# A decoder step on one core: mask DMAs issued from SyncE instead of GpSimd, and the sample attention placed later between the weight blocks

## The reference

```python
h = rmsnorm(x, g_mix); z = h @ w_in                   # q, k, v of three mixers, and merge gates
ya = mlstm(...)                                       # 4 heads
# B: dilated window attention, 3 groups x 2 heads; C: block-sparse attention, 6 heads
s = einsum('bthd,btjhd->bthj', q, keys) * Dh ** -0.5
s = where(idx >= 0, s + bias, -inf)                   # T5 bias by distance
p, lse = softmax_lse(s)
o = einsum('bthj,btjhd->bthd', p, values)
y = ga * (ya @ wa) + gb * (yb @ wb) + gc * (yc @ wc)  # ga, gb, gc = sigmoid(gates)
x = x + y @ w_out
x = x + (silu(a) * u) @ w_dn                          # a, u = split(rmsnorm(x) @ w_gu)
return rmsnorm(x, g_final)
```

## Time and profile before

| what | value |
|---|---|
| median of three runs | 1018.16 us |
| the profiled execution | 1017.9 us |
| its span, first to last instruction | 1016.0 us |
| outside the span | 1.9 us |
| PE busy | 994.9 us (98%) |
| weight loads on PE | 961.2 us (95%) |
| DVE, ACT, POOL busy | 49%, 34%, 7% |
| granted TensorE clock | 0.998 |
| mean DMA rate | 103 GB/s |

### The profile page before, as it was taken

One profiled execution on the slowest core, in us unless ns is written; L12 is line 12 of the kernel. 1 busy time (PEld: TensorE's weight loads), 2 busy tenths in 40 slices (PEclk: granted clock), 3 DMA queues, 4 the chain that ended last, 5 costly groups with the idle time before them and its releaser, 6 DMA issues.

```text
span 1016.0 us, 18552 instructions
## 1 busy us (share of the span) xinstructions
PE 994.9 (98%) x7715; PEld 961.2 (95%) x7715; DVE 494.5 (49%) x903; ACT 344.7 (34%) x579; POOL 69.1 (7%) x95
## 2 busy tenths in 40 slices
PE   6999999999999999999999999999999999999997
PEld 6799989998998889999999999999999999999997
DVE  5525456565587313263536556455545554332232
ACT  6434233444455343222322343232222222222122
POOL 0100014001100200020204000000000000000000
PEclk9999999999999999999999999999999999999999
DMA  7574345412121465422222222322222222222202
GB/s 254 166 287 99 48 141 90 166 54 84 56 84 42 127 184 162 125 84 84 84 84 84 84 84 98 103 91 84 84 83 84 83 84 93 94 85 73 91 25 88
DMA packets 104522, 104.17 MB, mean 103 GB/s; under 512 B 10825, under 2 KB 101379, under 8 KB 104199
## 3 DMA queue, kind: packets, MB, share of 16 engines
q1 hardware_dynamic: 101044, 91.94, 29.0%
q0 software_dynamic: 3344, 11.03, 3.3%
q10 hardware_dynamic: 52, 0.01, 0.0%
HBM read 97.16 MB, written 14.88 MB: 110 GB/s over the span
## 4 chain that ended last, share of the span: by engine, by line
PE 91%; DVE 3%; DMA 1%; POOL 1%; SPq 1%; issue 1%; ACT 1%; ACTq 0%; DVEq 0%; POOLq 0%
PE acc L432 75%; PE acc L936 3%; PE acc L916 2%; PE acc L999 2%; PE acc L926 1%; PE acc L1035 1%; POOL mt L751 1%; PE acc L982 1%; SPq L626 1%; PE acc L844 1%; PE acc L833 1%; DVE h_lo L1887 1%; PE acc L799 1%; DMA ring<-in_cache_dsa_kv 1%; DVE y_lo L1539 0%
## 5 line engine op out<-in xcount | busy, mean ns | idle before, releaser
L432 PE MATMUL acc<-h_hi,w_hi 128*128 128x256 f32 (+1 forms) x1520 | 472.3, 311 | 2.6 <-DVE w_lo L416 2.5
L432 PE MATMUL acc<-h_lo,w_hi 128*128 128x256 f32 (+1 forms) x1520 | 438.3, 288 | 0.0
L432 PE MATMUL acc<-h_hi,w_lo 128*128 128x256 f32 (+1 forms) x1520 | 436.7, 287 | 0.0
L432 PEld LDWEIGHTS acc<-h_hi,w_hi 128*128 128x128 f32 x1520 | 286.6, 189 | 13.9 <-issue 6.6
L432 PEld LDWEIGHTS acc<-h_lo,w_hi 128*128 128x128 f32 x1520 | 287.0, 189 | 6.5 <-issue 3.4
L411 ACT ACTIVATE w_hi<-raw 128x1024 fp32r<-128x1024 f32 x135 | 141.4, 1047 | 440.0 <-PE acc L432 439.9
L432 PEld LDWEIGHTS acc<-h_hi,w_lo 128*128 128x128 f32 x1520 | 286.7, 189 | 0.0
L416 DVE TENSOR_TENSOR w_lo<-raw,w_hi 128x1024 fp32r<-128x1024 f32 x135 | 165.4, 1225 | 111.1 <-ACT w_hi L411 106.5
L432 PE MATMUL acc<-s_hi,w_hi 128*128 128x256 f32 (+1 forms) x352 | 101.6, 288 | 0.0
L432 PE MATMUL acc<-s_lo,w_hi 128*128 128x256 f32 (+1 forms) x352 | 101.3, 288 | 0.0
L432 PE MATMUL acc<-s_hi,w_lo 128*128 128x256 f32 (+1 forms) x352 | 100.7, 286 | 0.0
(11 more groups left out here) (303 smaller groups left out, 1165.8 us busy)
## 6 DMA issues: line engine op xcount, KB each, us to landing
raw<-in_w_in SPq DMA_DIRECT2D x25, 1024.0 KB, 5.1
raw<-in_w_gate_up SPq DMA_DIRECT2D x22, 1024.0 KB, 4.9
raw<-in_w_down SPq DMA_DIRECT2D x8, 1024.0 KB, 5.1
ring<-in_cache_dsa_kv SPq DMA_DIRECT2D x4, 1024.0 KB, 6.5
raw<-in_w_out SPq DMA_DIRECT2D x4, 1024.0 KB, 5.0
out<-in_cache_dsa_kv SPq DMA_DIRECT2D x2, 2016.0 KB
rev<-tab POOLq DMA_DIRECT2D x1, 3840.0 KB, 34.7
ring<-in_cache_moba_k SPq DMA_DIRECT2D x48, 64.0 KB, 2.1
```

What stands on the lines that cost most here:

```text
L432: ins = nc.tensor.matmul(acc[:, bank, 0:HALF[half]], a[:, k, :], two(b[:, kx + k, :], half), start=first and k == k0 and c == 0, stop=last ...
```

## The change

Three things. The mask DMAs are issued by SP, between the fourth ring load and the next weight load, instead of by POOL. DVE's three operations that wait for them are due at T_SA + 1.6 instead of T_SA + 3.0. The due times of the sample attention are later and further apart, with those of its ring loads on SP, and the low parts of y have two due times instead of nine.

```diff
-        T_QK, D_QK = 1.3, 0.042
-        T_SM, T_P, D_PV = 3.4, 4.6, 0.05
+        T_QK, D_QK = 1.45, 0.048
+        T_SM, T_P, D_PV = 3.9, 5.05, 0.055
@@ SP
-                    when = (0.4, 0.41, 0.42, 0.43, 1.7, 2.05, 2.35, 2.7, 3.05, 3.4, 4.8, 4.9)
+                    when = (0.4, 0.41, 0.42, 0.43, 1.95, 2.35, 2.75, 3.1, 3.5, 3.85, 5.3, 5.4)
@@ SP, behind the issue of ring load n
+                        if n == 3:
+                            sp.wait_ge(sem("rev_out"), 16)
+                            for head in range(HEADS):
+                                half, q = divmod(head // 2, 3)
+                                w = P * NC4[head // 2]
+                                r0 = HD * half + TS * (head % 2)
+                                src = bass.AP(X["rev"].tensor, REV * head + TP - 1 - w,
+                                              [[4 * HEADS * REV, NB], [HEADS * REV - 1, TB], [1, w + TB]])
+                                sp.dma_start(S4[r0:r0 + TS, q, 2 * P - w:2 * P + TB], src
+                                             ).then_inc(sem("mask_in"), 16)
@@ POOL: the same loop taken out
-                for head in range(HEADS):
-                    ...
-                    pool.dma_start(S4[r0:r0 + TS, q, 2 * P - w:2 * P + TB], src).then_inc(sem("mask_in"), 16)
@@ DVE, merge
-                        yield T_SA + T_P + len(pv) * D_PV + (0.12, 0.12, 0.2, 0.2, 0.21, 0.4, 0.5, 0.6, 0.9)[i]
+                        yield T_SA + T_P + (0.12 if n < 2 else 0.2) + len(pv) * D_PV
@@ DVE, sample
-                    yield T_SA + T_SM - 0.4
+                    yield T_SA + 1.6
                     dve.wait_ge(sem("new_mm"), 1)
                     dve.wait_ge(sem("mask_in"), 16 * HEADS)
```

## The result

The changed kernel took 1031.61 us (median; 1030.99 to 1033.16) against 1018.03 (median of four runs of the kernel before): ratio 1.0138, 95% interval [1.012, 1.0154]. It is slower by 13.6 us, where 6.1 were forecast, and above the range. The direction and each wait's place were as forecast; the size wasn't. Its profiled execution took 1033.77, with a span of 1031.8.

A forecast was written before the change was run, and what follows sets the result against it. PE was taken as the bound (91% of the last-ending chain), its work plus gaps. Terms -0.5 + 5.0 - 1.0 + 0.1 - 0.4 + 3.4 gave +6.6, by position +5.6; +6.1 taken: 1017.9 + 6.1 = 1024.0 us, range 1019 to 1028.5.

The forecast's parts named there:

- the masks on SP: Scores, block 35: masks land at 367.4, so PE stalls before step 19 until 370.2; +5.0 us, bounds 2.0 to 10.1.
- Start, -0.5: First scores step, block 34: moved from place 5 to 8, weight work covers PE's 0.51 us ring-load wait; -0.5 us.
- Wider spacing, -1.0: Scores: 36 places instead of 32 among the steps, fewer steps directly following another; -1.0 us, bounds +0.3 and -4.2.
- Softmax, +0.1: Softmax: weight parts, a Tanh and an evacuation now ahead on ACT and DVE use about 1.3 of 1.6 us cover; +0.1 us.
- Values, -0.4: Products with the values: five places instead of four before the ninth step shorten PE's wait for the twelfth ring load; -0.4 us.
- y, +3.4: Last product with the values to PE's restart on y: chain 7.6 us, PE's work 3.0, gap 4.6 instead of 1.2; +3.4 us.
- What the masks delay on SP, "Nothing": SP's queue behind the masks: weights of blocks 39 and 40 and fifth and sixth ring loads go 5 us later, costing nothing.
- in time: Rival, scores: masks land by 362.4, no stall at step 19; +1.1 us, 1019.0; chance 0.15.
- spacing pays: Rival, scores: every step's key copy is ready and masks are in time; spacing gives -4.2 us, 1015.8; chance 0.07.
- SP is held behind its own loads: Rival, SP's queue: masks meet a hold-up like that behind the fifth ring load, landing 3.7 us later; 1027.7; chance 0.10.

The follow-up runs named there:

- masks_pool: The changed kernel with the twelve mask DMAs back on POOL, due times and early wait kept; 1020.9 us, ratio 1.0023 to the kernel before.
- The run with six masks: The changed kernel with six mask DMAs on SP and six on POOL, DVE waiting for all; 1029.01 us, ratio 1.0086 to the kernel before.
- the filled pair: On one chip, the changed kernel again (1032.84 us) and with 43 and 18 unread identity products in PE's waits for masks and y (1028.88 us).
- the two filled runs: The changed kernel with unread identity products in PE's waits for masks and y: 36 and 16 (1027.01 us), then 43 and 18 (1028.88 us).
- score_due_only: The kernel before with only the new due times of scores, softmax, values and ring loads; y's due times, masks and wait old; 1017.89 us, ratio 0.9988.
- the run with the late wait: The changed kernel with DVE's three mask operations due at T_SA + T_SM - 0.4 again, masks still on SP; 1024.44 us, ratio 1.0054 to the kernel before.

## Why the prediction was wrong

**The step that failed** is "the masks on SP", the term +5.0: the wait measured 9.43 us. Within it the price of an issue was wrong. The prediction took "an issue with no address register to set lies between 0.33 ... and 0.62 ... I take 0.45". It was 0.64, with pauses 0.70: outside the bounds that the rows had given. The 0.33 of SP's own rows came from loads of another shape; POOL's row, 0.58, was for the very same transfers and was the nearer one. Against the forecast, with the 1.7 of late start taken out:

- SP came to the masks 0.9 later (363.06 - 1.7 = 361.4 for 360.5). POOL's silence saved nothing: from its first paged load to the masks SP took 20.09 us, and 19.52 to the next weight load in masks_pool, where POOL issued them.
- The twelve starts spread over 7.7 instead of 4.95, 2.75 more.
- Landing took 2.4 for 2.0, the chain from there to PE 2.7 for 2.8.

The sum is 3.9, and step 19 came at 375.84 - 1.7 = 374.1 for the 370.2 on record. PE was there 0.5 sooner than forecast, hence the gap of 9.43. The run with six masks moved that gap by what six issues cost. The prediction's bounds for this wait alone, 2.0 to 10.1, held the 9.43, through a late landing that didn't come; the range for the time was narrower than they were.

The Trainium skill's rule (Trainium Kernel Development and Optimization, Key Constraints), that several issuing queues save only the sequencer's issue time, agrees with the runs: that issue time was 8.39 us here, and back on GpSimd the ratio fell from 1.0138 to 1.0023.

**The term that was missing**, put at nothing without a reason, is the clock: 3.3 us worked out, 3.7 between the rows of the filled pair and 3.8 between their ratios. The prediction priced its two new gaps by their own length alone. The Trainium skill's TensorE: Matmul & The Clock Gate, Part 1, says that the array's clock is gated by how busy the engine has been. The traces agree as far as the two filled runs go: with the engine at work in the waits the clock stayed at 1.00 at y in both and behind the masks in the second; in the first it fell there, behind the 2.16 us that were left.

The other terms:

- *Start, -0.5.* Right: no gap before L985.
- *Wider spacing, -1.0.* Right in sign but too small. In score_due_only the terms that apply (-0.5, -1.0, +0.1, -0.4, and y's 2.12 + 0.70 - 0.95 = +1.9) give +0.1; measured was -1.2, between -2.2 and -0.1. About 1 us more came from the spacing. In the changed kernel what is left for it is 12.7 - (9.43 + 3.3 + 3.56 - 0.51 - 0.61) = -2.5. These are remainders; no run shows the spacing by itself.
- *Softmax, +0.1.* The stage took 7.78 for 7.90.
- *Values, -0.4.* The gap was 1.11 for 1.3.
- *y, +3.4.* 4.51 - 0.95 = 3.56; the chain was 7.65 for 7.6, and the gap was 4.51 or 4.52 in five of the runs.
- *What the masks delay on SP, "Nothing".* True in the changed kernel, for a wrong reason: PE was held longer by the masks. With masks and fifth load in that order and no early wait, it is 2.8 to 4.1 us of gap. The argument had looked at the sixth load, not at the fifth, and had taken 5 us of delay where it was 9.1.

**The rivals.** Neither "in time" nor "spacing pays" came. "SP is held behind its own loads" (1027.7) was the nearest, and by another mechanism: each issue was slow, none was held up for long (the longest took 0.80). Its size and the missing clock together went past the range.

Put right, the sum is 6.1 + 3.9 + 3.3 = 13.3, less about 1 for the spacing: 12.3, against 12.7 in the stage and 13.6 between medians. What part of the remaining 0.9 is the early and late stretches of low clock, which differ from run to run, stays open.

## What to carry to other kernels

Before moving DMAs to a busier queue, price each issue by the row of that very transfer wherever it now stands, multiply by their number, and look at the next load behind them as well as at whoever waits for them. When a change opens a gap on TensorE, add to its length what the clock takes behind it, read from a matmul's spacing at either level (1.3 to 1.6 us and 2.1 us here, behind gaps of 9 and 4.5). A wait that is free where it stands, as DVE's early wait was with the masks on GpSimd, turns dear together with an edit that delays what it waits for.

## What the runs showed of the hardware

- A mask DMA (32 rows of up to 260 elements through a three-step pattern) took 0.643 us (median) to issue on SP in every kernel that had them there, a page of keys 0.333; on GpSimd the masks took 0.56 to 0.59. From the start of its issue the last one on SP landed in 2.3 us, and in before those from GpSimd in 4.4 (median). Whether the pattern, the rows or the target makes the 0.643 wasn't varied.
- The granted clock fell to 0.50 in or behind gaps of PE of 9.4, 5.2, 4.5, 4.5, 4.1, 2.2 and 1.9 us, and not behind one of 2.1 in score_due_only, nor the 2.78 of the run with the late wait. It stayed low until 3 to 5 us after PE was at work again. Which gap is just too long stays open.
- At 0.50 the 288-column matmuls started 0.24 apart for 0.13. Stretches of low clock at about 52 and in the last 15 us come and go between executions of one kernel.
